# First-layer modulation computed in quarters of matching shift and scale columns, with the condition loaded ahead of the other parameters

## What is computed

```
def _modulation(cond, w, b):
    m = jax.nn.silu(cond) @ w + b
    return jnp.split(m, 3, axis=-1)

shift, scale, gate = _modulation(c, ada_w[i], ada_b[i])
hx = _rmsnorm(x, norm_g[i]) * (1.0 + scale[:, None]) + shift[:, None]
cshift, cscale, cgate = _modulation(c_ctx, ada_w[i], ada_b[i])
hc = _rmsnorm(ctx, norm_g[i]) * (1.0 + cscale) + cshift
u, g = jnp.split(h @ w_in, 2, axis=-1)          # h is hx or hc; the pool mixer goes on from here
```

## Time and profile before

| | us |
|---|---|
| median of three runs | 1827.95 (1827.79 to 1828.08) |
| time of the profiled execution | 1828.98 |
| its span in the trace | 1827.2 |
| TensorE busy in the span | 1806.8 |

### The profile page before, as it was taken

How to read it: one execution, slowest core, us unless ns; L and a number is a source line. 1 busy time by engine, 2 the same in 40 slices (tenths; PEclk the granted TensorE clock), 3 DMA queues, 4 the chain that set the end, 5 groups by cost and what they waited for, 6 DMA issues and landing times.

```text
span 1827.2 us, 25144 instructions
## 1 busy us (share of the span) xinstructions
PE 1806.8 (99%) x9394; PEld 1491.3 (82%) x9394; DVE 916.0 (50%) x1690; ACT 911.6 (50%) x1351; POOL 1364.8 (75%) x568
## 2 busy tenths in 40 slices
PE   6999999999999999999999999999999999999999
PEld 5888788887889888887788888888888878888887
DVE  4673766778654524855553230713195565143152
ACT  3324524674456644456554644464445555545452
POOL 2624544559968898977689798969897868898885
PEclk9999999999999999999999999999999999999999
DMA  9852785739675675565465566557655645656653
GB/s 367 293 201 70 265 308 165 197 122 315 228 266 199 207 215 194 183 196 160 135 185 195 175 194 194 196 185 233 192 192 184 187 130 163 193 163 210 192 194 127
DMA packets 194841, 363.96 MB, mean 199 GB/s; under 512 B 32261, under 2 KB 48373, under 8 KB 194165
## 3 DMA queue, kind: packets, MB, share of 16 engines
q1 hardware_dynamic: 191856, 354.87, 60.9%
q10 hardware_dynamic: 2884, 7.73, 1.1%
HBM read 361.50 MB, written 6.10 MB: 201 GB/s over the span
## 4 chain that ended last, share of the span: by engine, by line
PE 98%; DMA 0%; DVE 0%; ACT 0%; ACTq 0%; issue 0%; POOL 0%
PE ps L1233 26%; PE ps L1235 26%; PE ps L1234 26%; PE ps L1359 3%; PE ps L1360 3%; PE ps L1361 3%; PE ps L1939 1%; PE ps L1940 1%; PE ps L1941 1%; PE ps L1281 1%; PE ps L1491 1%; PE ps L1866 1%; PE ps L1645 1%; PE ps L1616 1%; PE ps L1626 1%; PE ps L1911 1%
## 5 line engine op out<-in xcount | busy, mean ns | idle before, releaser
L587 POOL TENSOR_TENSOR w_lo<-raw,w_hi 128x1024 fp32r<-128x1024 f32 x556 | 1345.9, 2455 | 413.5 <-ACT w_hi L625 392.4
L1233 PE MATMUL ps<-w_hi,act_rows_r 128*128 128x512 f32 x2064 | 817.0, 396 | 3.8 <-POOL w_lo L587 3.1
L1235 PE MATMUL ps<-w_hi,act_rows_r 128*128 128x512 f32 x2064 | 806.0, 390 | 0.0
L1234 PE MATMUL ps<-w_lo,act_rows_r 128*128 128x512 f32 x2064 | 805.4, 390 | 0.0
L625 ACT ACTIVATE w_hi<-raw 128x1024 fp32r<-128x1024 f32 x556 | 571.4, 1058 | 357.1 <-DMA raw<-in_ffn_w_up 99.3
L1233 PEld LDWEIGHTS ps<-w_hi,act_rows_r 128*128 128x128 f32 x2064 | 388.5, 188 | 90.9 <-issue 8.8
L1235 PEld LDWEIGHTS ps<-w_hi,act_rows_r 128*128 128x128 f32 x2064 | 388.2, 188 | 81.8
L1234 PEld LDWEIGHTS ps<-w_lo,act_rows_r 128*128 128x128 f32 x2064 | 388.8, 188 | 76.8
L2584 DVE STREAM_TRANSPOSE ps<-proj 32x256 f32<-32x256 f32 (+1 forms) x384 | 166.6, 434 | 6.5
L2565 DVE TENSOR_TENSOR proj<-proj,ps 128x1024 f32<-128x1024 f32 (+1 forms) x18 | 20.4, 1133 | 252.2 <-PE ps L1235 247.8
L1359 PE MATMUL ps<-act_rows_r,w_hi 128*128 128x512 f32 (+1 forms) x288 | 101.4, 352 | 0.0
(11 more groups left out here) (243 smaller groups left out, 1557.2 us busy)
## 6 DMA issues: line engine op xcount, KB each, us to landing
raw<-in_w_in SPq DMA_DIRECT2D x120, 512.0 KB, 3.7
raw<-in_ffn_w_gate SPq DMA_DIRECT2D x88, 512.0 KB, 4.4
raw<-in_ffn_w_up SPq DMA_DIRECT2D x88, 512.0 KB, 4.4
raw<-in_ffn_w_down SPq DMA_DIRECT2D x88, 512.0 KB, 4.2
proj<-in_ada_w SPq DMA_DIRECT2D x39, 512.0 KB, 8.3
pt<-in_ada_w SPq DMA_DIRECT2D x38, 512.0 KB, 6.5
raw<-in_pool_w_in SPq DMA_DIRECT2D x32, 512.0 KB, 7.8
raw<-in_na_w_in SPq DMA_DIRECT2D x32, 512.0 KB, 5.7
```

The lines of the kernel that those rows point to most:

```text
L587: pool.tensor_tensor(w_lo[:, s, :], raw[:, s, :], w_hi[:, s, :].bitcast(F32), ALU.subtract).then_inc(lo_done, 1)
L1233: pe.matmul(o, h, hi, start=start, stop=False)
L1234: pe.matmul(o, h, lo, start=False, stop=False)
L1235: return pe.matmul(o, c, hi, start=False, stop=stop)
```

## The change

- The first four `ada_w` blocks are now quarters: quarter a holds the 256 shift columns and the 256 scale columns of the same features. Each of its four loads is split into two loads of 256 KB, with rows of 1 KB where they had 2 KB. `ADA_ORDER` goes.
- The conditions and the identity have their own semaphore (`cond_in`), are turned by a transpose of their own, and silu reads that in PSUM. The other parameters are staged in `bias` and split in two: the bias and norm gains before x, six others behind x. x is loaded as two loads, one a tile.
- SP sends half of quarter 0, weight group 0, the rest of quarter 0, quarter 1, group 1, ctx, quarter 2, group 2, quarter 3, group 3 and so on, and no longer waits for the parameters. POOL no longer waits for the gains.
- On DVE, each quarter is followed by the scaling and the low parts of unit q of tiles 0 and 1; the ctx units come between quarters 1 and 2, and after quarter 3. The orders of PE and ACT are rewritten to match.

```diff
-ADA_ORDER = (0, 2, 1, 3) + tuple(range(4, DEPTH * ADA_COLS))
@@ ada_weights
+                    if a < ADA_FIRST:
+                        for part in range(2):
+                            n0 = part * D + 256 * a
+                            sp.dma_start(free(ada_slot(k, a), [[512, 2], [1, 256]], 256 * part), v[:, 2 * k:2 * k + 2, n0:n0 + 256])                              .then_inc(ada_in[ada_place(a)][k], 16)
+                        continue
@@ narrow (SP)
+                        if stage == "p0_in" and g == 0:
+                            ada_weights(0, (2, 3))
+                            ada_weights(1)
                         if stage == "p0_in" and g == 1:
                             sp.dma_start(free(proj[:, 0:1], [[D, NT], [1, D]], CTX_RES),
                                          I["ctx"].rearrange("a (t p) d -> p (a t) d", p=P)).then_inc(ctx_in, 16)
                             ada_weights(2)
+                        if stage == "p0_in" and g == 2:
                             ada_weights(3)
@@ SP
-            ada_weights(0)
-            ada_weights(1, (0, 1))
-            sp.wait_ge(param_in, 16 * PARAMS)
-            ada_weights(1, (2, 3))
+            ada_weights(0, (0, 1))
@@ POOL
-            pool.wait_ge(dve_done, dve_s.count(("first_gains", 0, 1)))
@@ ACT
+            load(ident[:], I["ident"], cond_in)
+            for name, r in (("c", 0), ("c_ctx", 8)):
+                load(bias[r:r + 8, 0:P], bass.AP(I[name].tensor, 0, [[P, 8], [1, P]]), cond_in)
+            load(bias[0:96, P:2 * P], bass.AP(I["ada_b"].tensor, 0, [[P, 96], [1, P]]), param_in)
+            load(bias[96:128, P:2 * P], bass.AP(I["norm_g"].tensor, 0, [[P, 32], [1, P]]), param_in)
+            for t in range(NT):
+                load(x_res[:, t, :], I["x"].rearrange("a (t p) d -> p (a t) d", p=P)[:, t, :], x_in[t])
...
-            split(2)
-            for t in range(2 * NT):
+            for u in range(2, 4):
+                split(1)
+                for t in range(NT):
+                    high_of_tile("p0", t, some=(u,))
+            for t in range(NT, 2 * NT):
+                split(1)
                 high_of_tile("p0", t, half=1)
-                if t in (1, 2):
-                    split(1)
@@ PE start()
-                ada_products(0, 0)
-                ada_products(1, 1)
-                turn_half(0, 0)
-                turn_half(1, 0)
-                pe.wait_ge(ada_read, 2)
+                ada_products(0, 2)
+                for u in range(2):
+                    for t in range(NT):
+                        turn_unit(t, u)
                 part(0, 0)
+                ada_products(1, 3)
                 part(1, 0)
                 part(0, 1)
-                ada_products(2, 2)
+                part(1, 1)
                 turn_half(2, 0)
                 turn_half(3, 0)
...
+                ada_products(2, 2)
+                for t in (2, 3):
+                    read_out(bank_of(0, t))
+                    part(t, 0)
+                    part(t, 1)
+                turn_unit(0, 2)
+                pe.wait_ge(ada_read, 2)
                 ada_products(3, 3)
...
+                turn_unit(1, 2)
+                part(0, 2)
+                part(1, 2)
+                turn_unit(0, 3)
                 pe.wait_ge(ada_read, ADA_FIRST)
...
+                turn_unit(1, 3)
+                turn_half(2, 1)
+                part(0, 3)
+                turn_half(3, 1)
+                part(1, 3)
+                for t in (2, 3):
                     part(t, 2)
                     part(t, 3)
@@ PE
+            pe.wait_ge(cond_in, 48)
+            pe.transpose(ps[:, 4, 0:16], bias[0:16, 0:P], ident[0:16, 0:16]).then_inc(pe_done, pe_s.one("cond"))
@@ DVE
+            def first_units(q):
+
+                ada_block(q, 2 + q % 2)
+                first_gains(q)
                 for t in range(NT):
+                    full_units("p0", t, (q,), *modulated(0))
                 for t in range(NT):
+                    low_of_tile("p0", t, q, 2)
+
+            def ctx_units(half):
+
+                for t in range(NT, 2 * NT):
+                    full_units("p0", t, (half,), *modulated(0))
+                    low_of_tile("p0", t, half, 4)
+
+            first_units(0)
+            first_units(1)
             normed("p0", 2)
             normed("p0", 3)
+            ctx_units(0)
+            first_units(2)
+            first_units(3)
+            ctx_units(1)
```

More of the change, by code:

```diff
@@ L630, in load @@
                 act.dma_start(dst, src).then_inc(s, 16)
[L633 to L638, removed]
[L639 to L643 removed]
+            load(ident[:], I["ident"], cond_in)
[5 more added lines that the diff above has]
+                load(x_res[:, t, :], I["x"].rearrange("a (t p) d -> p (a t) d", p=P)[:, t, :], x_in[t])
+            for name, r, n in (("ffn1_norm_2", C_FFN1, 16), ("mix_norm_2", C_MIX, 16), ("ffn2_norm_2", C_FFN2, 16),
+                               ("pool_scale", C_PSCALE, 16), ("conv_dw", C_DW, 24), ("conv_db", C_DB, 8)):
+                load(bias[r:r + n, 0:P], bass.AP(I[name].tensor, 0, [[P, n], [1, P]]), param_in)
+            act.wait_ge(dve_done, dve_s.count("cond_zero"))
+            act.wait_ge(pe_done, pe_s.count("cond"))
+            act.activation(free(cond[:, 0:1, 0:1], [[1, 2], [32, KC]]), free(ps[:, 4, 0:1], [[8, 2], [1, 8]]), ACT.Silu).then_inc(act_done, act_s.one("cond"))
             def load_sqrt(k):
@@ L649, in rms @@
             def rms(key, t, src):
[L651 removed]
+                act.activation(free(proj[:, 0:1], [[1, D]], POOL_GATE + t * D), src, ACT.Square,
                                accum_out=stat[:, t:t + 1]).then_inc(act_done, act_s.one(("ss", key, t)))
@@ L2025, in ada_block @@
                 dve.wait_ge(ada_turned, a + 1)
-                dve.tensor_tensor(mods[:, to:to + 4, 0:n], free(ps[:, bank, 0:1], [[32, 4], [1, n]], P),
-                                  free(cols[:, 0:1], [[1, 4], [0, n]], C_ADAB + to), ALU.add).then_inc(ada_read, 1)
+                for at, to, some in ((0, 2 * a, 2), (2, 8 + 2 * a, 2)) if a < ADA_FIRST else ((0, 4 * a, 4),):
+                    last = dve.tensor_tensor(mods[:, to:to + some, 0:n], free(ps[:, bank, 0:1], [[32, some], [1, n]], P + 32 * at),
+                                             free(cols[:, 0:1], [[1, some], [0, n]], C_ADAB + to), ALU.add)
+                last.then_inc(ada_read, 1)
             def ada_summed(a, bank, between=None):
@@ L2091, in layer_gains, with first_gains @@
                 dve.wait_ge(dve_done, dve_s.count(("gains", l, 1 if l < 2 else 0)))
-            def first_gains(half):
-                dve.wait_ge(ada_read, 2 * half + 2)
-                at = 4 * half
-                for c in range(2):
-                    dve.scalar_tensor_tensor(
-                        out=gains[:, 0, c, at:at + 4], in0=mods[:, 8 + at:12 + at, c], scalar=1.0, in1=cols[:, C_NORMG + at:C_NORMG + at + 4],
-                        op0=ALU.add, op1=ALU.mult).then_inc(dve_done, dve_s.one(("first_gains", half, c)))
-                dve.wait_ge(dve_done, dve_s.count(("first_gains", half, 1)))
+            def first_gains(q):
+                dve.wait_ge(ada_read, q + 1)
+                dve.scalar_tensor_tensor(out=free(gains[:, 0:1, 0:1, 0:1], [[KC, 2], [1, 2]], 2 * q),
+                                         in0=free(mods[:, 0:1, 0:1], [[1, 2], [2, 2]], 2 * (8 + 2 * q)), scalar=1.0,
+                                         in1=free(cols[:, 0:1], [[0, 2], [1, 2]], C_NORMG + 2 * q),
+                                         op0=ALU.add, op1=ALU.mult).then_inc(dve_done, dve_s.one(("first_gains", q)))
+                dve.wait_ge(dve_done, dve_s.count(("first_gains", q)))
             def stream(t):
```

67 lines of the change are left out of this document (21 added, 46 removed).

## The result

The changed kernel takes 1833.61 us in the median of 20 runs (1830.79 to 1837.97), the kernel before 1828.42 in 20 runs beside it (1827.79 to 1834.28). The ratio is 1.0027, with a 95% interval of 1.0020 to 1.0033: 5.2 us slower by the medians. The profiled execution took 1834.37 us, with a span of 1832.3; that is 5.1 more in the span and 0.3 more outside it than before.

What follows compares the result with a forecast made beforehand. TensorE was taken as the bound, solidly busy after the first output block. That block's end, 19.8 + 30.4 + 6.3 + 1.3 = 57.8 against 55.66, put the median 2.1 us later, about 1830.0 us, range 1826.0 to 1832.5.

Steps and rivals of the forecast that it cites:

- The start of the first part: First matmul of the layer's product: to come at 19.8 us instead of 23.60, with x loaded ahead of six parameters.
- costs nothing and gains nothing: POOL's first low part: its wait for the gains could go without effect, since it lies beside the other work.
- The work behind it: TensorE from first part to block end: 30.4 us of work, 6.3 of waits and 1.3 for the clock.
- unit 1: After quarter 1, DVE needs 3.0 us while TensorE has one part of 1.38: a stall of 1.7.
- the new waiting: TensorE's handover stalls in the first output block: 6.3 us together, 0.8 before, so 5.5 us more.
- The block end: End of the layer's first output block: to come at 57.8 us instead of 55.66, 2.1 later.
- a solid body of TensorE work: All behind the first output block: untouched by the change, so the end moves by what the block end moves by.
- anything behind the first block that changed by more than a few tenths: Sign against the forecast: a change of that size in the program behind the first block would show it wrong.
- The handovers are hidden: Rival: DVE and ACT run ahead and the earlier start is kept; 3.9 us sooner, 1824.1; chance 0.08.
- The parameters come last and the clock stays low: Rival at the start: block end at 59.8 or a little more, 1832.1 us and up; chance 0.13.
- idle times shorter than 3.09 us bring no second fall: Granted clock in the first block: idle times at most 1.7 us, so no second fall; 1.3 us set for low clock.
- The half-size loads set the pace: Rival: 256 KB loads take as long as 512 KB ones; quarter 3 at 56, end 16 us later, 1844; chance 0.03.

Runs made afterwards that it cites:

- a_pool_wait: Changed kernel with POOL's wait for the first gains put back before its first low part; 1832.88 us, ratio 1.0023.
- b_no_pool_wait: Kernel before with only POOL's wait for the first gains removed; 1829.62 us, ratio 1.0008.
- a_orders: Changed kernel with POOL's wait back, quarter 1's product ahead of the first part, and turns for units 2 and 3 sooner on TensorE; 1828.67 us, ratio 1.0000.
- a_turns_early: Changed kernel with tile 1's turn for unit 2 ahead of quarter 3 and unit 3's turns one part sooner; 1834.62 us, ratio 1.0034.
- a_rel_later: Changed kernel with the second block's four bias-row copies (3 MB) sent after the attention stage's loop; 1831.71 us, ratio 1.0014.
- b_delay3: Kernel before with 27 idle transposes added on TensorE at the end of the first output block; 1832.57 us, ratio 1.0023.
- b_rel_later: Kernel before with the second block's four bias-row copies sent after the attention stage's loop; 1828.23 us, ratio 0.9999.
- b_halved: Kernel before with only its first sixteen `ada_w` loads each split into two of 256 KB with 1 KB rows; 1830.44 us, ratio 1.0011.
- a_wide: Changed kernel with the same 1 KB rows but neighbouring slots joined, 20 loads instead of 32; 1835.13 us, ratio 1.0031.
- a_early_split: Changed kernel with ACT's split of weight group 0 moved ahead of the squares of x; 1834.95 us, ratio 1.0027.
- a_orders_wide: Changed kernel with POOL's wait back, three reorderings on TensorE and loads joined to 20; 1827.55 us, ratio 0.9998.

## Why the prediction came out as it did

**The start of the first part (19.8, bounds 19.3 and 21.0; measured 21.12).** The parameters' transposes came at 13.20 where 12.8 was taken, and quarter 0 ended at 17.4 where 16.8 was. (Its matmuls ran at half the later pace, 32 weight loads in 1.48 us where the same take 0.81 at 33.17. The prediction calls that the low clock; the profile's clock column has 1.00 from 11 to 18 us.) What failed is the sentence that the removal of POOL's wait "costs nothing and gains nothing". The low part does lie beside the rest, but DVE's normed rows of tile 1 don't run beside it: 2.94 us instead of 0.75, so DVE could turn quarter 0 only at 18.44, 0.9 to 1.0 after it was ready. With the wait back, DVE turned it as soon as it was there (a_pool_wait), and the first part came 0.7 us sooner for it, as POOL's own low part then bounds it; b_no_pool_wait reproduced the hold-up in the kernel before. The wait that looked like an idle restriction had kept POOL off DVE's back.

The Trainium skill (SBUF — State Buffer, Who interferes with whom) states the rule that I should have weighed here: DVE and GpSimd share one pair of ports, whoever issues first holds it for the whole instruction and the other is fully blocked; it names `tensor_scalar` in a two-port mode and any DVE instruction with two SBUF inputs. The traces agree: the `TENSOR_SCALAR` ends 0.55 us after POOL's instruction (18.41 and 17.86), and the gain instruction with its two SBUF inputs takes 1.46 instead of 0.23. The order of the rows doesn't show who was first: DVE's row starts 0.04 us ahead of POOL's and is the one that was held.

**The work behind it (38.0 forecast, 37.5 measured).** The waits were rightly placed and a third too large: unit 1 1.17 (1.7 forecast), ctx tile 3 0.30 (0.8), first ctx part 0.19 (0.5), unit 2 1.25 (1.45), unit 3 1.30 (1.5), the last ctx ones none (0.35); 4.2 instead of 6.3. The rest, 37.5 - 4.2 = 33.3, is 2.9 over the 30.4 of pure work, where 1.3 was set for the clock. a_orders splits it: at full clock TensorE was busy for 29.57 us from its first part to the block end, in a stretch that the prediction's prices put at 28.5 (two quarters in it). So 1.1 of the 2.9 is work that was priced too low, and the other 1.8 is the clock, half from 21.0 to 24.4. The price was tested wrongly on the kernel before: the 0.8 us left over there were called short waits, but TensorE was busy for 31.99 of those 32.06 us. So the new waiting is 4.1 us where 5.5 was worked out. a_turns_early and a_orders confirm the waits: with other work put behind each handover they fall from 4.2 us to 1.7.

**The block end (57.8 forecast, 58.63 measured).** +2.1 was worked out, +3.0 was measured, and that it is so near is in part luck: 1.3 at the start, 1.1 of work and 0.5 of clock too little, 2.1 of waits too much. Had it been the only error, the median would have been at 1828.42 + 3.0 = 1831.4, within the range, and a_rel_later's is at 1831.71. (0.5 of the miss is the base: the forecast started from the 1827.95 of three runs, and the 20 runs beside the changed kernel gave 1828.42.)

**The end of the program.** The step that failed, and that put the time outside the range, is in the first paragraph: the rest of the program is "a solid body of TensorE work", "the change touches nothing in it", and "what it moves by, the end moves by". It touches no instruction there, but the body is not solid. In the attention stage small loads of the bias share a queue with large copies, and how long they take depends on when the stage meets them. This term stood at nothing in the sum, and it measured 1.9 us in the profiled execution and, by the medians, 5.2 - 3.0 = 2.2. b_delay3 shows it without any of the change's edits: 1.86 us in, 3.2 out. a_rel_later and b_rel_later show the cause: with the copies away, a shift of 3.4 goes in and 3.5 comes out, and both kernels' spread falls. A range that carried the shift of the block end over with an added 0 to 5 us would have held the time. The prediction did name this as a sign of being wrong: anything behind the first block that changed by more than a few tenths.

**The rivals.** "The handovers are hidden" was wrong for this order and right for another one (a_orders). "The parameters come last and the clock stays low" was wrong in both its parts: 0.4 us of lateness, and a granted clock of 0.94 where before had 0.58. But the prediction's argument on the clock, that idle times shorter than 3.09 us bring no second fall, isn't safe: in a_rel_later the clock fell at 28.7 behind idle times of 1.6 and 1.9 us. "The half-size loads set the pace" was wrong here, with no wait for a quarter, though b_halved shows the cost of 1.85 us where nothing covers it. (The formula that the prediction takes from the Trainium skill, DMA: Bandwidth & Descriptors, stands in its section Anatomy of one DMA — SWDGE (gpsimd) path, and was fitted on loads of that path; SP issues the loads here.) GB/s was 354 to 383 in the quarters, near the 370 named.

**Open.** Why the kernel before mostly escapes the loss in the attention stage: it too has the copies in the queue, and some of its runs do reach 1834.28. The longest landing doesn't tell the two apart: it is 8.2 us in the kernel before, in whose profiled execution TensorE lost nothing there, and 9.0 in the changed one.

```profile
DMA to landing us min/median/max: 2.2/2.6/8.2
```

The phase between the copies and the bias loads differs, but no run here varied it step by step. What sets where the half-clock stretch falls is open too. Nor was quarter 1 ahead of the first part run by itself, so a_orders' gain isn't split between its three edits and the clock.

## What to carry to other kernels

Ask of each wait that a change removes what it kept apart: a POOL instruction of 2.4 us that becomes free to start can hold a DVE instruction of four elements for all that time. When a long product is cut into pieces so that its first result comes sooner, each piece has a handover of its own (here 3 us), and the cut pays only if the order puts other matmuls behind each. And a shift at the start reaches the end unchanged only if no later stage is waiting on transfers at the edge: where the runs of the kernel before already spread upwards from a tight floor (here 1827.8 with single runs at 1834), look for that stage first.

## What was not expected of the hardware

- A DVE instruction with 128x4 operands in SBUF takes 0.16 us alone (two together 0.23), but two took 1.46 and one took 2.18 (at 38.34 in the changed kernel, beside a POOL instruction that starts at 38.11) while POOL ran its `w_lo` instruction of 2.35 to 2.40 us.
- Loads of 256 KB with 1 KB rows, in place of 512 KB with 2 KB rows, cost 1.85 us over 8.4 MB when on the path (b_halved). Joined to 20 loads where there were 32, with the same rows, they gave no gain (a_wide).
- Large copies in the same queue raise the longest landing of a 64 KB load from 3.4 us to 9.0, with the median only from 2.4 to 2.8. The profiled executions show a shift of 1.9 (changed kernel), 1.4 (b_delay3), 2.6 (b_halved), 2.8 (a_early_split), 3.7 (a_pool_wait), 4.4 (a_turns_early) and 0 (a_wide, a_orders, a_orders_wide) added in that stage.
- Executions of the same first block differ in when TensorE is held at half clock: from 21.0 to 24.4 us in the changed kernel, from 28.7 to 32.1 in a_rel_later. In a_pool_wait one more came in the attention stage, behind a wait of 2.1 us, and cost some 1.5.
